# Another shape for the products of a chunked recurrence, and another order of the values' products in attention

## The reference

```python
# RWKV-7 group, 8 heads x 64: for every token
sa = jnp.einsum('bhvk,bhk->bhv', S, -kk_t)
S = (S * w_t[:, :, None, :] + sa[..., :, None] * (kk_t * a_t)[:, :, None, :]
     + v_t[..., :, None] * k_t[:, :, None, :])
y = jnp.einsum('bhvk,bhk->bhv', S, r_t)
# MLA group, 8 heads: for every block of 128 queries
s = jnp.where(kpos[None, :] <= qpos[:, None], s, -jnp.inf)      # s = q k * scale
p = jax.nn.softmax(s, axis=-1)
o = jnp.einsum('bhqk,bkhd->bqhd', p, v)
```

## Time and profile before

| | us |
|---|---|
| median of 3 executions (1351.94 to 1355.68) | 1353.78 |
| the profiled execution | 1353.33 |
| its span, first to last instruction | 1351.5 |
| TensorE busy | 1315.0 (97%) |
| VectorE busy | 945.5 (70%) |
| ScalarE busy | 474.8 (35%) |
| GpSimd busy | 497.0 (37%) |

### The profile page before, as it was taken

How to read it: one execution, slowest core, us unless ns; L and a number is a source line. 1 busy time by engine, 2 the same in 40 slices (tenths; PEclk the granted TensorE clock), 3 DMA queues, 4 the chain that set the end, 5 groups by cost and what they waited for, 6 DMA issues and landing times.

```text
span 1351.5 us, 23894 instructions
## 1 busy us (share of the span) xinstructions
PE 1315.0 (97%) x9900; PEld 1071.2 (79%) x9900; DVE 945.5 (70%) x1110; ACT 474.8 (35%) x796; POOL 497.0 (37%) x323
## 2 busy tenths in 40 slices
PE   7999999999999989989999999999999999999997
PEld 6877677877776789986688878888888888888886
DVE  3657975257777634439677988877777787669877
ACT  3143643146555433334104522212222444333330
POOL 0000112001876210002084778766774354444030
PEclk9999999999999999999999999999999999999999
DMA  5111444779639952224222345444436986666562
GB/s 225 62 48 32 141 157 156 184 169 292 183 101 288 221 127 53 59 64 140 87 101 94 117 137 198 142 147 164 156 125 226 356 288 219 190 198 200 190 205 106
DMA packets 147372, 214.50 MB, mean 159 GB/s; under 512 B 79960, under 2 KB 86240, under 8 KB 146624
## 3 DMA queue, kind: packets, MB, share of 16 engines
q1 hardware_dynamic: 146976, 211.92, 49.3%
q10 hardware_dynamic: 288, 1.05, 0.2%
HBM read 137.89 MB, written 66.39 MB: 151 GB/s over the span
## 4 chain that ended last, share of the span: by engine, by line
PE 49%; DVE 3%; POOL 1%; issue 1%; ACT 1%; DVEq 0%; POOLq 0%; ACTq 0%
PE banks L2523 23%; PE banks L2410 18%; PE banks L2326 5%; PE banks L2398 2%; POOL tile_h L3083 1%; PE banks L2371 1%; DVE wout_lo L2736 0%; POOL tile_s L3083 0%; DVE y_all L2756 0%; DVE first_relu L2870 0%; PE banks L2352 0%; DVE gn_scale L2747 0%; PE banks L156 0%; PE banks L2337 0%; DVE yr_full L2762 0%
## 5 line engine op out<-in xcount | busy, mean ns | idle before, releaser
L2523 PE MATMUL banks<-stage_b_hi,stage_a_hi 128*128 128x512 f32 x448 | 174.3, 389 | 0.0
L2523 PE MATMUL banks<-stage_b_lo,stage_a_hi 128*128 128x512 f32 x448 | 174.3, 389 | 0.0
L2523 PE MATMUL banks<-stage_b_hi,stage_a_lo 128*128 128x512 f32 x448 | 174.3, 389 | 0.0
L2898 DVE TENSOR_TENSOR stage_a_lo<-stage_a_raw,stage_a_hi 128x1024 fp32r<-128x1024 f32 x56 | 97.7, 1745 | 35.2 <-ACT stage_a_hi L2665 35.2
L2665 ACT ACTIVATE stage_a_hi<-stage_a_raw 128x1024 fp32r<-128x1024 f32 x56 | 59.4, 1061 | 120.9 <-DMA stage_b_raw<-in_w_ffn 98.4
L2523 PEld LDWEIGHTS banks<-stage_b_lo,stage_a_hi 128*128 128x128 f32 x448 | 84.1, 188 | 17.6
L2523 PEld LDWEIGHTS banks<-stage_b_hi,stage_a_hi 128*128 128x128 f32 x448 | 84.1, 188 | 17.4
L2523 PEld LDWEIGHTS banks<-stage_b_hi,stage_a_lo 128*128 128x128 f32 x448 | 84.1, 188 | 17.3
L852 POOL TENSOR_TENSOR hT<-hT,rate 128x1024 f32<-128x1024 f32 x4 | 13.5, 3370 | 210.1 <-DVE kk_tile L773 210.1
L428 PE MATMUL banks<-xT_hi,win_hi 128*128 128x512 f32 x288 | 90.6, 396 | 0.0
L428 PE MATMUL banks<-xT_lo,win_hi 128*128 128x512 f32 x288 | 88.8, 389 | 0.0
(11 more groups left out here) (423 smaller groups left out, 3590.1 us busy)
## 6 DMA issues: line engine op xcount, KB each, us to landing
stage_b_raw<-in_w_ffn SPq DMA_DIRECT2D x50, 512.0 KB, 5.0
stage_a_raw<-hid_s SPq DMA_DIRECT2D x32, 512.0 KB, 4.0
w_landed<-in_w_ffn SPq DMA_DIRECT2D x30, 512.0 KB, 4.7
hid_s<-tile_s SPq DMA_DIRECT2D x60, 256.0 KB, 4.4
stage_a_raw<-hid_h SPq DMA_DIRECT2D x24, 512.0 KB, 4.0
hid_h<-tile_h SPq DMA_DIRECT2D x42, 256.0 KB, 2.0
win_raw<-in_w_in SPq DMA_DIRECT2D x20, 512.0 KB, 3.6
x_tok<-in_x SPq DMA_DIRECT2D x8, 512.0 KB, 7.6
```

What stands on the lines that cost most here:

```text
L2523: last = nc.tensor.matmul(ps[:, bank, :], s[a][:, j, tok], s[b][:, j, :], start=p == 0 and j == 0 and n == 0, stop=p == NP - 1 and j == 1 ...
L2898: V.tensor_tensor(s["a_lo"][:], s["a_raw"][:], s["a_hi"][:].bitcast(F32), ALU.subtract).then_inc(lo2, 1)
```

## The change

In the recurrence k and beta of a chunk stand side by side in one tile `bkb` (beta comes by two more transfers a chunk), and v and u in one tile `vu`, over all 128 rows. Products with both are then one: weights of 64 rows and 128 columns in the scores with r and in the transposes (`scores_step`, `transposes`), and weights of 128 rows and 64 columns in the state and in the outputs (`state_step`, `y_step`). The first chunk keeps its small products in scores and transposes. That makes 96 products a chunk. Some results move to other banks: X shares one with the k-kk scores, v with the first product.

```diff
@@ rwkv_chunks: the tiles and waits
-    bs = new("b_scores", tile, copies=2)
-    bk_tok = new("bk_tok", [P, 2, RT, CH], copies=2)
-    v_tok = new("v_tok", tile, copies=2)
-    u = new("u", tile)
+    bkb = new("beta_k_beta", [P, RT, 3, CH], copies=2)
+    rb = new("y_scores", [P, 2, RT, CH], copies=2)
+    kb_tok = new("kb_tok", [P, 2, RT, CH], copies=2)
+    vu = new("vu", [P, 2, RT, CH], copies=2)
+                if m >= 3:
+                    sp.wait_ge(tr_done, m - 1)
+                for p in range(2):
+                    sp.dma_start(bkb[m % 2][own[p], :, 2 - 2 * p, :], beta[own[p], :, now(m)])\
+                        .then_inc(beta_in[m % 2], 16)
@@ state_step and y_step, for each c
                     for p in range(2):
-                        mm(ps[own[p], B_SA, cols(c)], bk_tok[q][own[p], K, c, :], v_tok[q][own[p], c, :],
-                           start=True, stop=False)
-                    for p in range(2):
-                        last = mm(ps[own[p], B_SA, cols(c)], bk_tok[q][own[p], B, c, :], u[own[p], c, :],
-                                  start=False, stop=True)
+                        last = mm(ps[own[p], B_SA, cols(c)], kb_tok[q][:, p, c, :], vu[q][:, p, c, :],
+                                  start=True, stop=True)
...
                     for p in range(2):
-                        mm(ps[own[p], B_RY, cols(Y0 + c)], v_tok[q][own[p], c, :], ks[q][own[p], c, R, :],
-                           start=False, stop=False)
-                    for p in range(2):
-                        last = mm(ps[own[p], B_RY, cols(Y0 + c)], u[own[p], c, :], bs[q][own[p], c, :],
+                        last = mm(ps[own[p], B_RY, cols(Y0 + c)], vu[q][:, p, c, :], rb[q][:, p, c, :],
                                   start=False, stop=True)
@@ scores_step, chunks from 1 on
+                        if m:
+                            last = mm(ps[:, B_RB + p, cols(c)], bkb[q][own[p], c, 1 - p:3 - p, :], rd_now,
+                                      start=True, stop=True)
@@ the product X
+                    pe.wait_ge(ka_ready, m + 1)
+                    product(B_XA, prod, inv_t[z]).then_inc(xt_mm, 1)
@@ u_step and tokens_step on ScalarE: two halves instead of one operation
-                A(u[:], view(B_SA), ACT.Copy).then_inc(sa_ready, 1)
+                for p in range(2):
+                    A(vu[n % 2][other[p], p, :, :], ps[other[p], B_SA, 0:RT * CH].rearrange("p (c n) -> p c n", n=CH),
+                      ACT.Copy).then_inc(sa_ready, 1)
```

```diff
+    k.halves_of = ((0, 3), (1, 2))
@@ invert on VectorE
-                    step.mark(V.tensor_tensor(total[:], sums[:, 0, of], sums[:, 1, of], ALU.add))
+                    step.mark(V.reduce_sum(total[:], sums[:, :, of].rearrange("p m q -> p q m"), AX_X))
...
-                if h or g == EARLIER:
-                    dve.wait_ge(y_done[1 - g], h + g)
-                for c in range(2):
...
-                    last = V.tensor_tensor(inverse_diag[c][:], square, pair, ALU.mult)
+                if h:
+                    dve.wait_ge(y_done[g], h)
+                V.reciprocal(inverse_wide[g][:], row_sums.rearrange("p (j o) -> p j o", o=1).to_broadcast([P, 4, HD]))\
+                    .then_inc(inverse_ready[g], 1)
@@ TensorE's steps
+            EARLY_KTS = {1: (0, 1), 2: (2, 3)}
+                    if h and i in EARLY_KTS:
+                        pv(h - 1, EARLIER, EARLY_KTS[i])
                     if h and i == 3:
-                        pv(h - 1, EARLIER, (0, 1, 2, 3))
-                    if h and i == 4:
                         inverse_out(h - 1, EARLIER)
```

More of the change, by code:

```diff
@@ L1258, in inverse_out @@
                 pe.wait_ge(inverse_ready[g], h + 1)
-                for c in range(2):
-                    last = mm(ps[64 * c:64 * c + 64, BANK_Y + g, 2 * P:4 * P], ones[:, 0:HD],
-                              inverse_diag[c][:].rearrange("p j q -> p (j q)"), start=True, stop=True)
+                for j in range(2):
+                    for c in range(2):
+                        last = mm(ps[64 * c:64 * c + 64, BANK_Y + g, (2 + j) * P:(3 + j) * P],
+                                  inverse_wide[g][:, k.halves_of[c][j], :], ident[:], start=True, stop=True)
                 last.then_inc(y_done[g], 1)
@@ L1717, in sa_step @@
                     for p in range(2):
-                        last = mm(ps[own[p], B_SA, cols(c)], inv_t[n % 3][own[p], c, :], rhs[own[p], c, :],
+                        last = mm(ps[other[p], B_SA, cols(c)], inv_t[n % 3][own[p], c, :], rhs[own[p], c, :],
                                   start=True, stop=True)
@@ L1787, in transposes @@
                         v = hT[own[p], T_V + c, now(m)] if m else k.first_v[own[p], c, :]
-                        last = mm(ps[own[p], B_V, cols(c)], v, centre[own[p], :], start=True, stop=True)
+                        last = mm(ps[own[p], B_TV, cols(V0 + c)], v, centre[own[p], :], start=True, stop=True)
                 last.then_inc(tr_done, 1)
@@ L1824, in stage @@
                     y_step(n)
-            product(B_T1, low_t[0], inv[0]).then_inc(t1_mm, 1)
+            product(B_TV, low_t[0], inv[0]).then_inc(t1_mm, 1)
             scores_step(0)
```

146 lines of the change are left out of this document (79 added, 67 removed).

## The result

| us | before | after |
|---|---|---|
| median, before and after on one chip, 4 executions each | 1352.86 | 1393.18 (1391.11 to 1393.73) |
| span of the profiled execution | 1351.5 | 1391.7 |
| first right-hand side of the recurrence starts | 474.96 | 480.13 |
| stage 1 (chunk 0 finished, chunk 1 prepared) | 10.11 | 20.00 |
| stages 2 to 15, mean | 8.16 | 9.85 |

The account below looks back on a forecast made before the run. TensorE's products were taken to bound the recurrence (busy 96.75 of 100 us), with TensorE's chain of waits in attention. 1353.3 + 30 (recurrence) + 6.5 (attention) = 1390, rounded to 1389; range 1375 to 1401.

Parts of the forecast that it names:

- The price of a change of shape: TensorE drains 0.10 and exposes a load: 0.145 us into 64 columns of weights, 0.20 into 128; 20 changes a chunk.
- The chunk: One recurrence chunk on TensorE, summed step by step with the changes of shape: 9.75 us against 7.78.
- Stages 2 to 15: 14 recurrence stages go from 8.16 to 9.75 plus 0.2 for half of the earlier stalls: +25 us.
- Stage 1: Chunk 1's scores wait for two new beta transfers on SP until near 479.8; with its 20 changes, +4.6 us.
- Attention: All attention edits together, from early inverse, late halves, vanished stall and output transfers: +6.5 us, from -2 to +14.
- The early inverse: Attention: moved from step 4 to step 3 without products to cover it; TensorE stands 1.4 us, +9.1 over 7 heads.
- The stall of 3.65: VectorE's 128x4 add at 424.19 in attention goes with the one-operand sum: 2.1 of wait, 1.7 of clock, -3.8 us.
- The 2 us for SP's eight transfers: SP sends each head's attention outputs with 8 transfers of 0.61 instead of 4, delaying the stage's end: +2 us.
- the balanced halves: Attention: a second half's last column group becomes 256, 256, 128, 128 columns; saves 0.21 us a group, 0.43 a head.
- Free changes: First rival: changes among these recurrence shapes cost nothing, chunk 7.0 us, total 1348; chance 9%.
- hidden wide loads: Second rival: changes free and loads of 128 columns hidden too, chunk 6.2 us, total 1341; chance 4%.
- The third: Third rival: 128x64 pairs sharing all rows load one behind the other, 0.9 us more a chunk, total 1403; chance 6%.

Follow-up runs that it names:

- e3: The kernel after with products of one shape grouped in scores and y-step, same 96 products a chunk, fewer changes of shape: 1359.80 us, 1.0035 of before.
- e9: Attention of before; recurrence of after reordered to 4 changes of shape a chunk, solve beside first product, chunk 1's beta first on SP: 1337.68 us, 0.9889 of before.
- e4: The kernel after with chunk 1's two beta transfers issued ahead of all others of the recurrence on SP's queue: 1386.50 us, 1.0242 of before.
- e11: Recurrence of before, attention of after, but early values' products in step 3 and early inverse in step 4 as before: 1357.85 us, 1.0043 of before.
- e8: The kernel before with one edit: a late half's two row sums added by a reduction of one operand: 1350.85 us, 0.9995 of before.
- e12: e10 with e11's attention, and the recurrence's two first exponentials on ScalarE moved behind attention's last eviction: 1335.81 us, 0.9860 of before.
- e10: e9 with e8's sum of one operand, and 2 MB of values and gate transfers spread over chunks 3, 6, 9 and 12: 1332.36 us, 0.9849 of before.
- e6: Attention of before; recurrence of after with 64x64 scores and transposes, k and beta products alternating over four array quarters, 112 products a chunk: 1343.48 us, 0.9936 of before.
- e2: Attention of before with the recurrence of after: 1390.33 us, 1.0268 of before.

## Why the prediction was right, point by point

**The price of a change of shape** (0.10 of drain, 0.055 or 0.10 of exposed load). Right: the load starts 0.10 behind the last column, and e3 gives 0.142 a change by a count that uses no record's length, where the prediction's pairs have 0.148 (0.265 less 0.117) and 0.155 (0.373 less 0.218). The value was carried over from shapes with 128 rows or 32; that it holds for 64x64, 64x128 and 128x64 is now shown by the scores and the outputs of after. The rule of the Trainium skill (TensorEngine Tiling (Array Packing), Key Properties) that a change of mode drains the engine agrees with these 0.10.

**The chunk: 9.75 forecast, 9.77 measured.** Scores 2.40 against 2.50, y-step 2.12 against 2.10, right-hand side 0.94 against 0.95, transposes 1.03 against 1.04. The 0.10 missing in the scores is the solve's drain, counted one step later. The same prices gave 6.6 for e9, and 6.68 came. (In the prediction, 128 x 0.058 is 7.42; its 7.48 goes with half of 0.117.)

**Stages 2 to 15: +25 forecast, +23.6 measured.** The chunk is right, the 0.2 for stalls kept is wrong in kind. From stage 3 on there is none at all; stage 2 has 10.86, as its first us still run at the low clock. The stalls of before were not general noise: e3 at 48.8 records a us and e9 at 57.5 have none from stage 4 on either. That they belong to the density of records is argued, not shown.

**Stage 1: +4.6 forecast, +9.9 measured; the term that was mis-sized.** The mechanism, chunk 1's scores behind the beta transfers, is right. The wait ended at 484.94 instead of 479.8, since the whole stage and SP's queue with it started late (beta issued at 482.07, not 476.3). Its size is right too: 2.7 more ahead of the scores, where 479.8 less 477.05 is 2.75, and e4 without it is 2.6 shorter. What was left out is the clock behind it: 10.11, 2.7 of wait and 2.0 for the chunk's own growth give 14.8, so 5.2 of the 20.0 are left for 15 us at half clock. In e4 the executions with the higher clock are 5.6 to 7.8 shorter than the others. The prediction had considered such a fall for attention only.

**Attention: +6.5 forecast, +5.2 by the first right-hand side; part of this is luck.** The early inverse waits 1.46 where 1.4 was worked out, in five heads of seven; in e11's trace the move is worth 9.25 by the last head, against 9.1, of which the tail and the clock behind it take half back. The wide reciprocal takes 1.74 to 1.75 (1.75 forecast). The stall of 3.65 and the low clock behind it are gone, but through two edits together, which the prediction did not see: e8 with the new sum alone gains nothing. The 2 us for SP's eight transfers are near in size and wrong in their way. The outputs themselves account for 0.4 at most (TensorE stands 1.27 ahead of the next part instead of 0.86). The wait in the tail is 2.72, where before had none for ScalarE. The reload of beta and cum is late, ScalarE stands 4.85 for it, and head 7's last probabilities are queued behind on that engine.

The sum for attention (its terms add up to 6.7) is right only in its total. By head 7's late inverse after is 1.4 behind before (its load at 468.02 against 466.60, rows below), where the sum has 4.7, and e11, without the move, is 8.0 ahead (458.62), where the sum's other terms give 4.4. About 3.4 was worked out for the balanced halves (0.43 a head, eight heads) and put into no sum, and fits the gap; no run tests it by itself. The dearer tail makes up for it.

```profile
466.60 0.20 PEld L1260 LDWEIGHTS banks<-verse_sums_diagonal,ones_full 128*64 128x64 f32 x4 [0.33 <-DVE verse_sums_diagonal L1475]
```

```profile
468.02 0.42 PEld L1267 LDWEIGHTS banks<-ident,inverse_sums_wide 128*64 128x64 f32 x8 [1.55 <-DVE inverse_sums_wide L1478]
```

**The rivals.** Free changes (1348) and hidden wide loads (1341) are refuted by the chunk. The third, 128x64 pairs that load one behind the other (1403), falls too: eight such products take 0.56 to 0.62 with a drain, where the serial case would need 0.9 more a chunk for its sixteen. The rule of the Trainium skill (TensorE: Matmul & The Clock Gate, The mechanism) on overlapping loads, which would have given this case, disagrees with these rows.

So 1389 was off by 4. Stage 1 was 5.3 too short and the end 1 too short; stages 2 to 15 and attention were together 2.7 too long, and 1 was lost in the rounding of 1390. The price of a change and the chunk were right by their mechanism; that the total came so close is in part luck: the clock and the tail's wait were left out or too small, the stalls kept and the missing halves pull the other way.

## What to carry to other kernels

Before products are merged into larger tiles, count the changes of shape in TensorE's order, not the products: at about 0.14 us a change, the fourteen that e3 takes out had cost 1.9 us of a chunk of 9.8. Taking them out, and nothing else, brought the kernel from 3% slower than before to 0.35%; e9, with four changes and the solve beside the first product, is 1.1% faster than before. Read the rate from distances between starts in a timeline; the busy share went up here while over a third fewer records ran in the same time. When engines are made faster at the end of a stage, look at the queue that issues the next stage's transfers: in e12 they were done sooner and nothing was gained, as that queue was not free.

## What the runs showed of the hardware

- Four quarters of the array in turn: 64x64 products with 64 columns, alternating between a quarter and its neighbour in the same rows, take 0.033 to 0.036 each (16 in 0.52 in e10, 0.57 in e6), where two quarters give 0.058.
- Products of 64x128 with 64 columns, in a group, take 0.12 each (e10), as much as two of 64x64 in two quarters; products of 128x64 take 0.07 with the drain behind eight of them (0.56 in e3).
- A recurrence of such short products reached 60 to 64 records a us over twelve stages in four kernels, with stalls that have no releaser in the trace; at 57.7 (e10) there were none. That the supply of instructions is the limit is argued from this, not shown.
- An operation of VectorE with two operands stood for 3 us and more beside GpSimd's copy (3.65 for a 128x4 add, 3.81 for two 128x256 multiplications), while reductions and reciprocals of one operand kept their 0.15, 0.18 and 1.75.
- TensorE's clock went to half for 10 to 15 us in stage 1 of the profiled executions of after, e2, e3 and e4, in e4 without the wait for beta. Two other executions of e4 have a mean clock of 0.998 and 0.995, so it need not. In before, with idle loads of 1.08 and 1.37 at the same place, it stayed at full.
